# Forget-gate sums of a forgetting attention carried by the second score product, placed by DMA, in a hybrid decoder block

## The chip, the cores and the metric

One core of a Trainium2 chip runs the whole layer. The metric is the device time of one execution in microseconds; lower is better. The engines are TensorE (PE in the profile, PEld for its weight loads), VectorE (DVE), ScalarE (ACT), GpSimd (POOL) and SyncE (SP), which issues all DMAs. The PE clock granted over the profiled execution was 0.996 of full speed.

## The reference

A layer of width 1024 over 512 tokens: an RMS norm, one input projection, three mixers (a gated linear recurrence, a "native sparse" attention NSA, a forgetting attention FOX), an output projection and the residual. In all score products head_dim is 64 and queries and keys are RMS-normalised per head. What the change touches is the FOX score:

```python
log_f = jax.nn.log_sigmoid(f_logits.astype(jnp.float32) + f_b.astype(jnp.float32))
c = jnp.cumsum(log_f, axis=1).transpose(0, 2, 1)
...
s = (jnp.einsum('bqhd,bshd->bhqs', qb, k).astype(jnp.float32) * ATTN_SCALE
     + cb[..., None] - c[:, :, None, :])
p = safe_softmax(s, mask)
```

The term of the query's own position, cb, is the same for all keys of a row and falls out of the softmax; the kernel adds only the keys' term, minus c.

## The kernel before, in words

**Projections.** The input weights come in 39 chunks of 128 output channels (`CHUNKS`), the output weights in 12 more. SP loads each into a ring of three (`raw`, `load_w`, L435), ACT rounds it to float32r (`wh`, L552), DVE writes the remainder (`wl = raw - wh`, `split_low`, L922), both in rings of four slots, three chunks ahead of PE. PE computes each chunk as three products over eight k tiles (L1351, L1352, L1355; the token-major value chunks L1318 to L1320). The three chunks vn0 to vn2 are one projection, which waits for the low split of all three. The order of chunks is a list; FOX's queries (fq), keys (fk) and values (vf) and the gate chunks zn follow after the NSA attention, the chunks zf after the FOX attention.

**Head norms.** For a query or key chunk ACT squares, PE averages over heads, ACT seeds the root and DVE finishes it (`norm`, L941 to L943). Then ACT writes the high part (L626) and DVE the low part (`low_parts`, L952). A head has 64 channels, so one half of the 128 partitions is its own: the tile `q_fox` holds high queries in that half and low queries in the other. For keys both `kh_fox` and `kl_fox` are filled in the own half, and SP copies each into the other half by DMA (`stack`, L445). One product with `kh_fox` then gives (high + low query) times high key, one with `kl_fox` the same times low key.

**The forget gates.** ACT writes the log gates of 8 heads beside the table `head_sel`; `forget_gates` on DVE (L979 to L987, in chunk zn1) sums them along the tokens and splits the sum into three bf16 parts in `c_parts`, at partitions 0, 32 and 64. `head_sel` (built by `attention_tables`, L1205 to L1208) has ones in the three rows of a head, so a third product of `head_sel` and `c_parts` adds the sum of a head to all rows of its scores.

**The attentions.** The work is cut into units: one head, one query tile of 128, n = (t+1) x 128 keys. Eight units, two heads by four tiles in the order t = 1, 2, 0, 0, 3, 1, 2, 3, are a pair; the NSA attention has eight pairs, FOX four. Per unit PE computes the scores (FOX: L1482, L1483, L1484; NSA: L1483, L1484) into one of four banks (`S_RING`), DVE adds the mask and finds the maximum (L1143), ACT the exponential (L721), DVE the reciprocal of the sums, POOL scales (`scale_probs`, L529), PE transposes five units later (L1492), ACT or DVE copies that back, and PE multiplies with the values (L1511). Scores of unit u wait for the exponential of unit u - 4.

**The order on SP.** One loop over c issues the load of chunk c once the low split of chunk c - 3 is done, and after it the stacking of chunk c - 6; what stands behind a wait in this queue waits with it.

**DVE around chunks nq1 and nq2** (81 to 95 us). After the second compress (`compress(1)`, L1426, which signals `cmp_prod`) DVE finishes the norm of nq1, splits weights, writes low queries, and runs steps of the recurrence (L1006 to L1011), all elementwise operations of 128x512 or 64x512. POOL has no work there; its next is the first scale of the NSA attention.

## Time and profile before

| | |
|---|---|
| the runs shown | 429.39, 430.83 and 1045.02 us, median 430.83 |
| profiled execution | 429.14 us, of which span 427.4 us |
| PE, DVE, ACT, POOL busy | 97%, 67%, 61%, 16% of the span |
| NSA attention | 138.7 to 202.1 us |
| FOX projections and norms | 202 to 300.6 us |
| FOX attention | 300.6 to 334.2 us |
| last projections, output | 334.2 to 427.4 us |

The page of the profile gives busy shares and the chain of work that ended last; the timeline gives each instruction's start and time; the waits say who released an idle engine. Matmuls overlap in the records: the distance between two starts says more than their durations. A busy PE is therefore not PE at its peak.

### The profile page before, as it was taken

Reading aid. Unit: us, or ns where it says so; the run is one execution under the profiler, and the core shown is the slowest. Engines: PE = TensorE matmul, PEld = TensorE weight load, DVE = VectorE, ACT = ScalarE, POOL = GpSimd, SP = SyncE. Lnnn points to the kernel's source line nnn. Section 1 sums busy time; section 2 is a strip of 40 time slices with the busy share of each in tenths; the row PEclk is TensorE's granted clock in tenths of the full one; section 3 lists DMA queues with packets and bytes.
Section 4 is the critical chain, followed back from the end, with each engine's and each line's share of the span. In section 5 each row is a group of like instructions: output and inputs, shape, how many; then the busy total and the mean of one; then the engine's idle time right before and its main releaser. Section 6 shows DMA issues by size and latency. Waiting matters only on the chain.

```text
span 427.4 us, 6574 instructions
## 1 busy us (share of the span) xinstructions
PE 416.0 (97%) x2254; PEld 327.7 (77%) x2254; DVE 287.2 (67%) x616; ACT 258.8 (61%) x514; POOL 67.4 (16%) x125
## 2 busy tenths in 40 slices
PE   6999999999999899998999999999999999999996
PEld 4876788779888766665777987988776688888885
DVE  4667759988898876766268846799877389522205
ACT  5746996686565887885187778751877654311100
POOL 6000000000000656566000000000465200000000
PEclk9999999999999999999999999999999999999999
DMA  8912544421122000001112333641300115822005
GB/s 284 338 72 97 152 114 108 121 76 38 55 95 99 2 2 1 1 2 61 43 55 89 100 98 117 180 133 66 99 2 2 49 51 181 278 99 83 2 0 196
DMA packets 12385, 38.89 MB, mean 91 GB/s; under 512 B 1728, under 2 KB 1984, under 8 KB 12096
## 3 DMA queue, kind: packets, MB, share of 16 engines
q1 hardware_dynamic: 12352, 38.47, 28.0%
q8 instruction: 18, 0.29, 0.3%
q14 instruction: 15, 0.12, 0.1%
HBM read 32.17 MB, written 2.10 MB: 80 GB/s over the span
## 4 chain that ended last, share of the span: by engine, by line
PE 83%; DVE 9%; issue 2%; ACT 2%; POOL 2%; DMA 1%; SPq 0%; ACTq 0%; DVEq 0%
PE bank L1351 12%; PE bank L1355 12%; PE bank L1352 12%; PE bank L1511 6%; PE bank L1492 6%; PE bank L1599 5%; PE bank L1600 5%; PE bank L1601 5%; PE bank L1483 3%; PE bank L1484 3%; PE bank L1405 2%; PE bank L1318 2%; PE bank L1320 2%; PE bank L1319 2%; DMA raw<-in_w_in 1%
## 5 line engine op out<-in xcount | busy, mean ns | idle before, releaser
L1351 PE MATMUL bank<-xh,wh 128*128 128x512 f32 x248 | 103.0, 415 | 0.6 <-DVE wl L922 0.6
L1355 PE MATMUL bank<-xh,wl 128*128 128x512 f32 x248 | 96.9, 391 | 0.0
L1352 PE MATMUL bank<-xl,wh 128*128 128x512 f32 x248 | 96.8, 390 | 0.0
L922 DVE TENSOR_TENSOR wl<-raw,wh 128x1024 fp32r<-128x1024 f32 (+1 forms) x51 | 61.5, 1207 | 37.0 <-ACT wh L552 36.6
L552 ACT ACTIVATE wh<-raw 128x1024 fp32r<-128x1024 f32 (+1 forms) x51 | 52.6, 1037 | 29.3 <-PE bank L1601 28.4
L1351 PEld LDWEIGHTS bank<-xh,wh 128*128 128x128 f32 x248 | 46.6, 188 | 15.9 <-issue 6.3
L1143 DVE CUSTOM_DVE_ANT_0 bank<-bank,mask_row 128x256 f32<-128x256 f32 (+3 forms) x96 | 46.8, 500 | 14.8 <-PE bank L1484 14.1
L1352 PEld LDWEIGHTS bank<-xl,wh 128*128 128x128 f32 x248 | 46.6, 188 | 11.5 <-issue 2.6
L1355 PEld LDWEIGHTS bank<-xh,wl 128*128 128x128 f32 x248 | 46.5, 188 | 10.1
L529 POOL TENSOR_SCALAR probs<-probs,rcp,gates 128x384 f32<-128x384 f32 (+3 forms) x44 | 28.4, 655 | 138.5 <-DVE rcp L1167 138.5
L721 ACT ACTIVATE probs<-bank,negmax 128x256 f32<-128x256 f32 (+3 forms) x64 | 33.6, 529 | 6.4 <-DVE negmax L1143 6.1
L1600 PE MATMUL bank<-wl,yh 128*128 128x512 f32 x96 | 37.4, 389 | 0.0
L1599 PE MATMUL bank<-wh,yh 128*128 128x512 f32 x96 | 37.4, 389 | 0.0
L1601 PE MATMUL bank<-wh,yl 128*128 128x512 f32 x96 | 37.4, 389 | 0.0
L731 ACT ACTIVATE pT<-bank 128x384 f32<-128x384 f32 (+1 forms) x48 | 26.1, 545 | 14.9 <-PE bank L1492 14.4
L1492 PE MATMUL bank<-cst,probs 128*128 128x128 f32 x160 | 28.5, 277 | 2.1 <-POOL probs L529 1.1
L1318 PE MATMUL bank<-wh,xh 128*128 128x256 f32 (+1 forms) x96 | 29.1, 303 | 0.0
L1319 PE MATMUL bank<-wl,xh 128*128 128x256 f32 (+1 forms) x96 | 27.6, 287 | 0.0
L1320 PE MATMUL bank<-wh,xl 128*128 128x256 f32 (+1 forms) x96 | 27.5, 287 | 0.0
L1483 PE MATMUL bank<-kh_nsa,q_nsa 128*128 128x256 f32 (+3 forms) x64 | 25.0, 393 | 0.6 <-ACT probs L721 0.6
L1492 PEld LDWEIGHTS bank<-cst,probs 128*128 128x128 f32 x160 | 18.5, 140 | 7.2 <-POOL probs L529 3.9
L1601 PEld LDWEIGHTS bank<-wh,yl 128*128 128x128 f32 x96 | 18.0, 188 | 3.8
(233 smaller groups left out, 764.6 us busy)
## 6 DMA issues: line engine op xcount, KB each, us to landing
raw<-in_w_in SPq DMA_DIRECT2D x36, 512.0 KB, 3.4
raw<-in_w_out SPq DMA_DIRECT2D x12, 512.0 KB, 3.4
x_raw<-in_xT SPq DMA_DIRECT2D x4, 512.0 KB, 7.1
x_res<-in_x_tok SPq DMA_DIRECT2D x1, 2048.0 KB, 9.5
out_y<-y_out SPq DMA_DIRECT2D x8, 256.0 KB, 2.2
raw<-in_w_in SPq DMA_DIRECT2D x3, 384.0 KB, 3.2
cmp_w_sb<-in_cmp_w SPq DMA_DIRECT2D x1, 1024.0 KB, 7.2
kh_fox<-kh_fox SPq DMA_DIRECT2D x8, 128.0 KB, 2.3
```

What stands on the lines that cost most here:

```text
L552: act.activation(wh[:, c % HL, 0:width(c)], raw[:, c % RAW, 0:width(c)], ACT.Copy).then_inc(wh_ready, 1)
L922: dve.tensor_tensor(wl[:, c % HL, cols], raw[:, c % RAW, cols], wh[:, c % HL, cols].bitcast(F32), ALU.subtract).then_inc(wl_ready, 1)
L1143: dve.tensor_tensor_reduce(scores, scores, mask_row[:, SEQ - n:], scale=-1.0, scalar=3.0e38, op0=ALU.add, op1=ALU.min, accum_out=negmax[:, ...
L1318: pe.matmul(dst, xh[:, k, toks], hi[:, k], start=(k == 0), stop=False)
L1351: pe.matmul(dst, hi, xh[:, k, :], start=(k == 0), stop=False)
L1352: pe.matmul(dst, hi, xl[:, k, :], start=False, stop=False)
L1355: mm = pe.matmul(dst, lo, xh[:, k, :], start=False, stop=(k == KT - 1))
L1483: pe.matmul(dst[:, 0:n], q, kh[:, 0:n], start=(group == "nsa"), stop=False)
L1492: mm = pe.transpose(PT[u % PTB][:, cols], probs_of(u, j * P, (j + 1) * P), ident)
L1599: pe.matmul(dst, yh[:, e, toks], wh[:, c % HL, cols], start=(e == 0), stop=False)
L1600: pe.matmul(dst, yh[:, e, toks], wl[:, c % HL, cols], start=False, stop=False)
L1601: mm = pe.matmul(dst, yl[:, e, toks], wh[:, c % HL, cols], start=False, stop=(e == ET - 1))
```

## The change

The separate product of `head_sel` and `c_parts` in a FOX unit goes. The sums are now split into three float32r parts in `c_rows`. In the second product the moving tile `kl_fox` keeps low keys in the head's own half; its other half is zeros but for three rows, which hold the head's three sums. The stationary side is no longer `q_fox` but a second tile with the high query in its own half and, in the other, ones in those three rows and zeros elsewhere. So low query times low key is no longer computed.

The second query tile of heads 0 and 1 (and later 6 and 7) is the new `q_first`; heads 2 to 5 use slots 1 and 2 of the weight ring `wl`, which are free between chunks zn2 and zn3 and the chunks zf2 and zf3. POOL fills zeros and ones by copies of one column: eight fills of `kl_fox`, four of `q_first`, after `cmp_prod` reaches 2. SP copies the queries (`place_queries`) and the sums (`place_c`, eight DMAs of three rows, stepping 32 partitions in `c_rows`); low keys of FOX are no longer stacked. PE waits for `c_placed` in place of `c_ready` and for `q_placed` at each pair's first unit.

```diff
@@
 OUT_ORDER = (2, 1, 0, 3)
+Q_SLOT = {1: N_IN - 2, 2: N_IN - 1}
 STACK_LAG = 6
...
         ones = mask_row[:, SEQ - P:]
-        head_sel_f = sb("head_sel_f", [P, HEADS * P], BF16)
-        head_sel = head_sel_f[0:96, :].rearrange("p (h q) -> p h q", h=HEADS)
-        log_f = head_sel_f[96:96 + HEADS, :].bitcast(F32)
-        c_parts = sb("c_parts", [96, SEQ], BF16)
+        c_rows = sb("c_rows", [P, SEQ], F32R)
+        log_f = c_rows[96:96 + HEADS, :].bitcast(F32)
         rstd_bc = sb("rstd_bc", [P, SEQ])
...
                 kl_fox = sb("kl_fox", [P, HEADS, SEQ], F32R, m)
+                q_first = sb("q_first", [P, 2, SEQ], F32R, m)
             with ExitStack() as m:
...
-            return sum(0 if CHUNKS[x][0] in ("nq", "fq") else 4 for x in NORMED[:c])
+            return sum({"nq": 0, "fq": 0, "fk": 2}.get(CHUNKS[x][0], 4) for x in NORMED[:c])
...
             return slice(s * HD, (s + 1) * HD)
+        def const_rows(s):
+            return slice((1 - s) * HD, (1 - s) * HD + 3)
+        def query_and_ones(h):
+            if h // 2 in Q_SLOT:
+                return wl[:, Q_SLOT[h // 2] % HL, h % 2 * SEQ:(h % 2 + 1) * SEQ]
+            return q_first[:, h % 2, :]
...
             return q_fox[:, h, :], kh_fox[:, h, :], kl_fox[:, h, :]
+        def low_query(u):
+            group, h, _, _ = unit(u)
+            return query_and_ones(h) if group == "fox" else q_nsa[:, h, :]
...
                     own, other = half_of(s), half_of(1 - s)
-                    for plane in key_planes(c, s):
+                    planes = key_planes(c, s)
+                    for plane in planes[:1] if CHUNKS[c][0] == "fk" else planes:
                         sp.dma_start(plane[other, :].bitcast(F32), plane[own, :].bitcast(F32)).then_inc(stacked, 16)
+            def place_queries(i):
+                sp.wait_ge(h_ready, 2 * nth_normed(AT["fq", i]) + 2)
+                if i == 0:
+                    sp.wait_ge(cmp_prod, 2)
+                elif i in Q_SLOT:
+                    sp.wait_ge(fox_consts, HEADS + 4)
+                    sp.wait_ge(proj_done, proj_units(Q_SLOT[i] - HL + 1))
+                else:
+                    sp.wait_ge(s_ready, NSA_UNITS + PAIR_UNITS)
+                for s in range(2):
+                    own, other = half_of(s), half_of(1 - s)
+                    dst = query_and_ones(2 * i + s)
+                    sp.dma_start(dst[own, :].bitcast(F32), q_fox[own, 2 * i + s, :].bitcast(F32)).then_inc(q_placed[i], 16)
+                    if i in Q_SLOT:
+                        sp.dma_start(dst[other, :].bitcast(F32), q_first[other, s, :].bitcast(F32)).then_inc(q_placed[i], 16)
+            def place_c():
+                sp.wait_ge(c_ready, 1)
+                sp.wait_ge(fox_consts, HEADS)
+                for h in range(HEADS):
+                    sp.dma_start(kl_fox[const_rows(h % 2), h, :].bitcast(F32),
+                                 c_rows[h:h + 65:32, :].bitcast(F32)).then_inc(c_placed, 16)
...
             for c in range(4, N_STREAM + 6):
+                if c == N_IN - 1:
+                    place_c()
                 load_w(c)
+                if c == N_IN:
+                    for i in range(1, HEADS // 2):
+                        place_queries(i)
                 k = c - 5
...
                     stack(k)
+                if k == AT["fq", 0]:
+                    place_queries(0)
                 if c == N_IN + 4:
...
             pool.wait_ge(sel_set, NT + 1)
-            nc.gpsimd.memset(c_parts[:, :], 0.0)
             nc.gpsimd.memset(k_cmp[:, :, :], 0.0)
...
+            def fill(dst, rows, src):
+                return nc.gpsimd.tensor_copy(dst[rows, :], src[rows, 0:1].broadcast_to([rows.stop - rows.start, SEQ]))
+            def zeros_and_ones(h):
+                s = h % 2
+                fill(query_and_ones(h), half_of(1 - s), mask_row).then_inc(fox_consts, 1)
+                pool.wait_ge(fox_consts, HEADS + 2 * h + 1)
+                fill(query_and_ones(h), const_rows(s), one1).then_inc(fox_consts, 1)
+            pool.wait_ge(cmp_prod, 2)
+            for h in range(HEADS):
+                fill(kl_fox[:, h, :], half_of(1 - h % 2), mask_row).then_inc(fox_consts, 1)
+            zeros_and_ones(0)
+            zeros_and_ones(1)
             pool.wait_ge(gates_ready, 1)
...
                 one, b = std[96:96 + HEADS, :], work[0:HEADS, :]
-                mid = std[0:HEADS, :].bitcast(BF16)[:, 0:SEQ]
+                mid = std[0:HEADS, :].bitcast(F32R)
                 dve.wait_ge(normed, len(NORMED))
                 link(dve.tensor_tensor_scan(b, one, log_f, 0.0, ALU.mult, ALU.subtract))
-                dve.wait_ge(small_consts, 2)
-                link(dve.tensor_copy(c_parts[0:HEADS, :], b))
-                link(dve.tensor_tensor(b, b, c_parts[0:HEADS, :], ALU.subtract))
+                link(dve.tensor_copy(c_rows[0:HEADS, :], b))
+                link(dve.tensor_tensor(b, b, c_rows[0:HEADS, :].bitcast(F32), ALU.subtract))
                 link(dve.tensor_copy(mid, b))
-                link(dve.tensor_tensor(b, b, mid, ALU.subtract))
-                dve.tensor_copy(c_parts[32:32 + HEADS, :], mid)
-                dve.tensor_copy(c_parts[64:64 + HEADS, :], b).then_inc(c_ready, 1)
+                link(dve.tensor_tensor(b, b, mid.bitcast(F32), ALU.subtract))
+                dve.tensor_copy(c_rows[32:32 + HEADS, :], mid.bitcast(F32))
+                dve.tensor_copy(c_rows[64:64 + HEADS, :], b).then_inc(c_ready, 1)
...
-                sel = work[0:96, 0:HEADS]
-                link(dve.tensor_tensor(sel, cst[0:96, IDENT:IDENT + HEADS], cst[0:96, IDENT + 32:IDENT + 32 + HEADS],
-                                       ALU.add))
-                link(dve.tensor_tensor(sel, sel, cst[0:96, IDENT + 64:IDENT + 64 + HEADS], ALU.add))
-                dve.tensor_copy(head_sel[:, :, :],
-                                sel.unsqueeze(2).broadcast_to([96, HEADS, P])).then_inc(sel_ready, 1)
                 dve.tensor_copy(mask_row[:, SEQ - P:], cst[:, CAUSAL:CAUSAL + P])
...
                 dst, q = SCORE[u % S_RING], q[:, t * P:(t + 1) * P]
-                if group == "fox":
-                    pe.matmul(dst[:, 0:n], head_sel[:, h, :], c_parts[:, 0:n], start=True, stop=False)
-                pe.matmul(dst[:, 0:n], q, kh[:, 0:n], start=(group == "nsa"), stop=False)
-                pe.matmul(dst[:, 0:n], q, kl[:, 0:n], start=False, stop=True).then_inc(s_ready, 1)
+                if group == "fox" and u % PAIR_UNITS == 0:
+                    pe.wait_ge(q_placed[h // 2], 16 * (4 if h // 2 in Q_SLOT else 2))
+                pe.matmul(dst[:, 0:n], q, kh[:, 0:n], start=True, stop=False)
+                pe.matmul(dst[:, 0:n], low_query(u)[:, t * P:(t + 1) * P], kl[:, 0:n],
+                          start=False, stop=True).then_inc(s_ready, 1)
...
             pe.wait_ge(normed, len(NORMED))
-            pe.wait_ge(c_ready, 1)
+            pe.wait_ge(c_placed, 16 * HEADS)
+            pe.wait_ge(fox_consts, HEADS + 4)
             attention(NSA_UNITS, UNITS)
```

GpSimd behind the last of the small memsets, before:

```order
L509 MEMSET kv_pair 128x2x512
L513 COPY kv_pair<-chn 128x16 [waits chan_loaded,pe_placed]
L513 COPY kv_pair<-chn 128x16
L520 MEMSET u_pad 128x3 [waits x_sq_act,x_sq,xl_ready]
L520 MEMSET u_pad 128x3 x3
L529 TENSOR_SCALAR probs<-probs,rcp,gates 128x256 [waits rcp_ready,gates_ready]
```

and with the change, at the same place (`mask_row` is zero in its first column, `small` holds the one):

```order
L568 MEMSET u_pad 128x3 [waits x_sq_act,x_sq,xl_ready]
L568 MEMSET u_pad 128x3 x3
L583 CAST kl_fox<-mask_row 64x512 [waits cmp_prod]
L583 CAST kl_fox<-mask_row 64x512 x7
L583 CAST q_first<-mask_row 64x512
L583 CAST q_first<-small 3x512 [waits fox_consts]
L583 CAST q_first<-mask_row 64x512
L583 CAST q_first<-small 3x512 [waits fox_consts]
L577 TENSOR_SCALAR probs<-probs,rcp,gates 128x256 [waits rcp_ready,gates_ready]
```

Twelve casts now stand between the pads of the recurrence and the first scale; they wait only for the second compress.

SyncE from the stacking of the last key chunk to the loads behind the FOX attention, before:

```order
L445 DMA kh_fox<-kh_fox 64x512
L445 DMA kl_fox<-kl_fox 64x512
L435 DMA raw<-in_w_in 128x1024 [waits wl_ready] x4
L435 DMA raw<-in_w_out 128x1024 [waits wl_ready] x5
L479 DMA x_res<-in_x_tok 128x4096 [waits proj_done]
```

and with the change:

```order
L451 DMA raw<-in_w_in 128x1024 [waits wl_ready] x3
L486 DMA kl_fox<-c_rows 3x512 [waits fox_consts,c_ready]
L486 DMA kl_fox<-c_rows 3x512 x7
L451 DMA raw<-in_w_in 128x1024 [waits wl_ready]
L451 DMA raw<-in_w_out 128x1024 [waits wl_ready]
L477 DMA wl<-q_fox 64x512 [waits proj_done,fox_consts,h_ready]
L479 DMA wl<-q_first 64x512
L477 DMA wl<-q_fox 64x512
L479 DMA wl<-q_first 64x512
...
L477 DMA q_first<-q_fox 64x512 [waits s_ready,h_ready]
L477 DMA q_first<-q_fox 64x512
L451 DMA raw<-in_w_out 128x1024 [waits wl_ready] x4
```

The eight small copies stand ahead of the last load of input weights, the copies of queries behind the first load of output weights.

TensorE at the first two units of the FOX attention, before:

```order
L1482 MATMUL bank<-c_parts,head_sel_f 128x256 [waits c_ready,normed,p_ready,stacked,l_ready]
L1483 MATMUL bank<-kh_fox,q_fox 128x256
L1484 MATMUL bank<-kl_fox,q_fox 128x256
L1482 MATMUL bank<-c_parts,head_sel_f 128x384 [waits p_ready]
L1483 MATMUL bank<-kh_fox,q_fox 128x384
```

and with the change:

```order
L1411 MATMUL bank<-xh,wl 128x512
L1539 MATMUL bank<-kh_fox,q_fox 128x256 [waits fox_consts,c_placed,p_ready,normed,q_placed0,stacked,l_ready]
L1540 MATMUL bank<-kl_fox,q_first 128x256
L1539 MATMUL bank<-kh_fox,q_fox 128x384 [waits p_ready]
L1540 MATMUL bank<-kl_fox,q_first 128x384
```

A unit has two products instead of three, and the first one waits for the DMAs.

## Rows read from the trace of the kernel before

**Rows 1.** The page, part 4: the chain that ended last, shares by engine.

```profile
PE 83%; DVE 9%; issue 2%; ACT 2%; POOL 2%; DMA 1%; SPq 0%; ACTq 0%; DVEq 0%
```

**Rows 2.** Busy time by stretch: length, PE, PEld, DVE, ACT, POOL, clock, DMA.

```profile
45.00:90.00 45.00, 45.00 (x203) 35.76 (x196) 35.33 (x54) 35.93 (x57) 0.00 (x0) 1.00 0.44 120
...
317.90:326.50 8.60, 8.60 (x62) 6.30 (x61) 6.22 (x26) 6.36 (x21) 4.78 (x8) 1.00 0.00 0
```

**Rows 3.** The bias product by line: ns min/median/max, first and last start, forms.

```profile
L1482 PE MATMUL bank<-c_parts,head_sel_f x32: 222/305/389, 300.6 to 328.7; 96*128 96x256 bf16 x8, 96*128 96x384 bf16 x8, 96*128 96x128 bf16 x8, 96*128 96x512 bf16 x8
```

**Rows 4.** Chain in order of time: start, share, what; a product of 512 columns.

```profile
309.67 0.23 PE bank L1484
```

**Rows 5.** Timeline of PE: start us, us; first products of pairs, and two last ones.

```profile
143.61 0.36 PE L1483 MATMUL bank<-kh_nsa,q_nsa 128*128 128x256 f32 x1
...
151.17 0.39 PE L1483 MATMUL bank<-kh_nsa,q_nsa 128*128 128x256 f32 x1
...
157.12 0.48 PE L1483 MATMUL bank<-kh_nsa,q_nsa 128*128 128x512 f32 x1
...
158.88 0.39 PE L1483 MATMUL bank<-kh_nsa,q_nsa 128*128 128x256 f32 x1
...
300.66 0.36 PE L1483 MATMUL bank<-kh_fox,q_fox 128*128 128x256 f32 x1
...
305.98 0.36 PE L1483 MATMUL bank<-kh_fox,q_fox 128*128 128x256 f32 x1
...
313.53 0.37 PE L1483 MATMUL bank<-kh_fox,q_fox 128*128 128x256 f32 x1
...
322.10 0.37 PE L1483 MATMUL bank<-kh_fox,q_fox 128*128 128x256 f32 x1
...
328.77 0.58 PE L1483 MATMUL bank<-kh_fox,q_fox 128*128 128x512 f32 x1
```

**Rows 6.** Waits, 143.6 to 200 us: us in total, times, longest.

```profile
PEld bank L1483 <- ACT probs L721: 3.9, 8, 0.8
```

**Rows 7.** Timeline of DVE and POOL, 331 to 333 us; POOL's forms in 309.4 to 326.5.

```profile
331.31 0.69 DVE L1105 TENSOR_TENSOR qr<-qr,sq 128x512 f32<-128x512 f32 x1
331.49 1.04 POOL L529 TENSOR_SCALAR work<-work,rcp,small 128x384 f32<-128x384 f32 x1 [0.65 <-DVE rcp L1167]
332.03 1.03 DVE L1107 TENSOR_TENSOR o_nsa<-qr,o_nsa 128x512 f32<-128x512 f32 x1
...
L529 POOL TENSOR_SCALAR probs<-probs,rcp,small 128x384 f32<-128x384 f32 x4 | 2.6, 661 | 2.3 <-DVE rcp L1167 2.3
L529 POOL TENSOR_SCALAR probs<-probs,rcp,small 128x512 f32<-128x512 f32 x3 | 2.3, 767 | 0.7 <-DVE rcp L1167 0.7
```

**Rows 8.** Timeline: the last product of the compress, DVE behind it, the vn projection.

```profile
80.92 0.34 PE L1426 MATMUL bank<-kv_pair,cmp_w_sb 128*128 128x96 f32 x1
...
81.45 0.75 DVE L943 SCALAR_TENSOR_TENSOR qr<-qr,chn,std 128x512 f32<-128x512 f32 x1
...
85.97 1.22 DVE L1011 TENSOR_TENSOR_SCAN u_pad<-tau,ig 128x512 f32<-128x512 f32 x1
88.17 0.69 DVE L899 TENSOR_TENSOR qr<-bank,rstd_bc 128x512 f32<-128x512 f32 x1 [0.97 <-PE bank L1355]
...
93.65 0.96 DVE L922 TENSOR_TENSOR wl<-raw,wh 128x768 fp32r<-128x768 f32 x1
...
94.67 0.40 PE L1318 MATMUL bank<-wh,xh 128*128 128x288 f32 x1
```

**Rows 9.** Timeline of DVE: the end of the forget sums, the first FOX reduction.

```profile
295.38 0.42 DVE L987 CAST c_parts<-work 8x512 bf16<-8x512 f32 x1
...
301.43 0.42 DVE L1143 CUSTOM_DVE_ANT_0 bank<-bank,mask_row 128x256 f32<-128x256 f32 x1
```

**Rows 10.** SP's timeline at a stacking; DMA issues: KB each, us to landing.

```profile
249.03 0.60 SPq L445 DMA_DIRECT2D kh_fox<-kh_fox  x1
249.67 0.60 SPq L445 DMA_DIRECT2D kl_fox<-kl_fox  x1
...
kl_fox<-kl_fox SPq DMA_DIRECT2D x8, 128.0 KB, 2.3
```

More of the change, by code:

```diff
@@ L220, in program @@
         lam_act, csp_ready = sem("lam_act"), sem("csp_ready")
-        zl_sig, zl_done, sel_ready = sem("zl_sig"), sem("zl_done"), sem("sel_ready")
+        zl_sig, zl_done = sem("zl_sig"), sem("zl_done")
         ones_ready = sem("ones_ready")
@@ L232, in program @@
         sq_ready, norm_mean, norm_seed = sem("sq_ready"), sem("norm_mean"), sem("norm_seed")
+        c_placed, q_placed, fox_consts = sem("c_placed"), [sem(f"q_placed{i}") for i in range(HEADS // 2)], sem("fox_consts")
         normed, h_ready, l_ready, stacked = sem("normed"), sem("h_ready"), sem("l_ready"), sem("stacked")
@@ L676, in place_log @@
                 act.wait_ge(log_T, 1)
-                act.wait_ge(sel_ready, 1)
                 for t in range(NT):
```

## The prediction

> **What bounds the kernel now.** I read the page first: its chain of work that ended last lies to 83% on PE [rows 1], so a microsecond counts where PE waits or where PE's own work shrinks. Then the busy times by stretch. In a pair of the forgetting attention (317.9 to 326.5 us) PE is busy throughout while DVE, ACT and POOL are busy 6.2, 6.4 and 4.8 of 8.6 us; between 45 and 90 us PE is busy throughout and POOL does nothing [rows 2]. So the attention is near PE's limit, but three quarters of the way to ACT's, and every stall put into the projections before it is paid in full.
>
> **The attention: what goes.** Thirty-two bf16 matmuls, one ahead of each fox unit's two float32r products, are removed [rows 3]. They cover 8 x 20 x 128 / 2 = 10,240 columns (a pair's eight units have 20 blocks of 128, four pairs); a product of 512 columns holds the chain 0.23 us [rows 4], so PE's own saving is at most 20 x 0.23 = 4.6 us. The least is nothing. The kernel holds its own measurement of what is left: the NSA units do exactly what a fox unit will do (two products, same tiles, same transposes, values, reductions, exponentials). Starts of a pair's first product: NSA 143.61, 151.17, 158.88, so 7.56 and then 7.71; fox 300.66, 305.98, 313.53, 322.10, so 5.32, 7.55 and 8.57 [rows 5]. The first two fox stretches are filling, set by DVE, ACT and POOL, and already at NSA's pace: gain 0. The third gives 8.57 - 7.71 = 0.86. From the first to the last product of the last pair fox takes 328.77 - 322.10 = 6.67 and NSA 157.12 - 151.17 = 5.95: 0.72. Sum 1.6 us gained of the 4.6. What is late next is the ring of four score banks: in six NSA pairs PE's loads waited 3.9 us for the exponential that frees one [rows 6]. I take 1.6; ends 0 and 4.6.
>
> **The fills on POOL: the largest term.** Twelve casts of up to 64x512 are put on POOL behind cmp_prod, that is from about 81.3 us, when the second compress ends. POOL is idle there, so by itself this costs nothing; nor is any later POOL work late (the first scale waits until after 140 us). But the fills read and write SBUF while DVE runs through operations with two SBUF inputs. The trace shows what such pairs do to each other: at 331.31 DVE multiplies two SBUF tiles; POOL's 128x384 scale issued at 331.49 takes 1.04 us instead of 0.66, and the next DVE product, issued at 332.03, takes 1.03 instead of 0.69 [rows 7]. So each POOL read holds such a DVE operation by about 0.34 us for 384 elements, 0.34 x 512 / 384 = 0.45 for 512, and they alternate. POOL's fill should run between its 384 and 512 forms, 0.66 to 0.77 us [rows 7].
>
> Where it lands: from 81.45 to 87.19 us DVE runs seven such operations (L943, L922, L952 twice, L1009, L1010, L1011), then idles 0.97 us until PE has finished chunk nq2 [rows 8]. Seven fills delay it 7 x 0.45 = 3.2, of which the idle takes 0.97: 2.2 pass through. Of the five fills left, three find operations with one SBUF input (L899, L1023, L941, 1.7 us in all), two delay L942 and L943: 0.9. From 88.17 on DVE runs without a gap to the low split of chunk vn2 at 93.65, which ends at 94.61, and PE starts the vn projection, which needs it, at 94.67 [rows 8]: no slack at all. So 2.2 + 0.9 = 3.1, taken as 3.0, go straight into PE's chain; nothing behind it gives them back, since DVE and PE shift together. The ends: 0, if a cast that reads one column of a tile does not hold DVE; and if POOL's twelve go through in one row with DVE standing, the whole time of 12 x about 0.6 = 7.2, less 0.97, is 6.3 us.
>
> The Trainium skill (SBUF — State Buffer, section "Who interferes with whom") says the pair of ports that both engines share is an exclusive lock, taken for the whole instruction, when DVE has two SBUF inputs and GpSimd reads SBUF. The trace agrees that one blocks the other, but not on the length: 0.34 us of an operation of 0.66. With whole instructions the nine delays would be about 0.66 each, 5.9 less 0.97, so 5 us in place of 3.0. The same section says a GpSimd instruction that only writes does not contend; the memset of c_parts that goes is of that kind and is worth nothing here.
>
> **The sums' way to PE.** Before, DVE wrote c_parts in place at 295.38 + 0.42 = 295.80 [rows 9], and PE's first fox unit came at 300.66 [rows 5]. Now the last sum is about 0.13 later (a float32 copy in place of a bf16 one of 0.28), then SP issues eight DMAs of 3 x 512, and PE waits for all eight. SP's copies within SBUF start 0.64 us apart and land 2.3 us after issue [rows 10]. No row shows one of three partitions. If it costs as much, the eighth issues at 295.95 + 7 x 0.64 = 300.4 and lands at 302.7: PE stands 2.1 us. Since DVE's first reduction starts only at 301.43 [rows 9], some 0.4 after its scores, the attention itself slips 1.7. If issues take half and landing 2.0, the eighth lands at 300.2 and it is 0. I take 1.3, nearer the row; ends 0 and 2.1.
>
> Behind place_c in SP's queue stand the loads of chunk 38 and of the first w_out chunk. They leave 1 to 3 us later, but are not read before the next split after the attention, some 30 us on: free. Behind them stand the four copies for heads 2 and 3, with one megabyte of loads ahead of them in the same queues. Issued from about 302.3 in steps of 0.64, the last leaves at 304.2 and lands at 306.5; the second pair, at 305.98 before, is now due near 307. Close, so I charge 0.3 us (ends 0 and 1). Heads 4 and 5 are due 7 us later, heads 6 and 7 sixteen: free. place_queries(0) waits for the high parts of fq0, which ACT writes before DVE's low split that the next load needs anyway: free. The next weight load, of w_out 1, waits for a split after the attention: SP's new wait for the first pair's scores costs it nothing. Eight stacking copies of the low keys go; PE did not wait for them: nothing. On DVE the three operations that built head_sel, near 47 us, go, 1 us at most under a PE that is busy throughout there [rows 2]: nothing.
>
> **Sum.** +3.0 (fills) + 1.3 (sums) + 0.3 (queries) - 1.6 (matmuls) = +3.0 us. The profiled execution took 429.14 us (427.4 of span and 1.7 around it), so it would be 432.1. Two of the three runs shown took 429.39 and 430.83, the third, 1045.02, stands alone; their middle is 430.1, 0.7 below the median, and 430.1 + 3.0 gives 433.1. I say 433.0.
>
> **Rivals.** (A) Not slower: the fills cost nothing. The place is DVE at 81.3 to 88.2 us; the mechanism is that POOL's casts from a single broadcast column read little, or that POOL always yields, so that DVE is held less than the 0.97 us of idle ahead of 88.17. From that point on the term is 0 and the sum is 0.0: 430.1, and if the placement is cheap too, 428.5. For it: no row shows a cast with such a source, and a delay of under 0.14 per fill would do. Against it: [rows 7]. (B) POOL wins the port each time, since its next fill is queued when DVE's operation asks; the term is 6.3 instead of 3.0: 436.4. For it: eight fills have no wait among them. Against: in [rows 7] the two take turns. The skill's rule on whole instructions leads to about the same place, 435.1. (C) The attention is PE-bound and gives the whole 4.6: 430.1 again, by another way. Against it: ACT needs 6.4 of the 7.4 us that would be left per pair and NSA pairs stall on it [rows 2, 6]. (D) The placements are late by more than their rows say (eight small copies and four queries behind a megabyte of loads), 3 us more: 436.1. For it: each has one semaphore and PE waits for the last. Against: copies of 128 KB land in 2.3 us.
>
> **How the numbers follow.** Forecast 0.40, A 0.25, B 0.18, C 0.07, D 0.10. The forecast's own range is 431.5 to 434.5. A and C reach down to 428.5 and 430, B and D up to 436.4, both together to 439.5. From 429.0 to 437.0 leaves out the lower tail of A and the sum of B and D, under 0.2. Two per cent, about what a measurement of this kernel can tell from no change, is 8.6 us: slower by more needs B and D together (439.5), 0.06; faster by more would need 422, beyond the 4.6 us that are there, 0.02; within it 0.92.
>
> **What would show it.** Right: POOL fills at 81 to 90 us with DVE operations of two SBUF inputs at 1.1 instead of 0.69 us beside them; DVE's idle of 0.97 gone; PE standing some 3 us in all before 98 us, and the vn projection starting near 97.7 instead of 94.67. Attention: PE idle 1 to 2 us before the first fox unit with c_placed as releaser; fox pairs 7.7 apart in the third stretch. Wrong: vn starting at 94.7 (A), fox pairs at 7.3 (C), DVE operations of several us beside the fills (B), or PE waiting for a DMA at the start of the second pair by more than a microsecond (D).

## The result, and the profile after

| | before | after |
|---|---|---|
| median of 6 runs each, us | 430.36 | 433.05 |
| lowest to highest of the six, us | 429.39 to 1045.02 | 432.35 to 433.65 |
| profiled execution: time, span, us | 429.14, 427.4 | 433.3, 431.5 |
| granted clock, mean over the profiled span | 0.996 | 0.984 |

The ratio after to before is 1.0073, with the 95% interval 1.0055 to 1.0092: about 3 us slower (the interval is 2.4 to 4.0 us), within the 2% called no change. The run of 1045.02 us stands alone and has no known cause; without it the median before is 430.29, and the medians are 2.8 us apart. The forecast was 433.0. The total came out, and none of its four terms did: the fills were put too high, the sums, the queries and the gain too low. First the chain of the page, which stays on PE [rows 1], with 4% of issue where 2% stood:

```profile
PE 82%; DVE 8%; issue 4%; ACT 2%; POOL 2%; DMA 1%; POOLq 0%; SPq 0%; ACTq 0%; DVEq 0%
```

The main reading is PE's timeline (start in us, length, line, operation, in brackets the idle time before it and its releaser):

```profile
94.60 0.28 PE L1607 MATMUL bank<-cst,v_cmp 64*32 64x64 f32 x2
96.64 0.40 PE L1374 MATMUL bank<-wh,xh 128*128 128x288 f32 x1 [1.75 <-DVE wl L985]
...
141.46 0.36 PE L1539 MATMUL bank<-kh_nsa,q_nsa 128*128 128x256 f32 x1
...
303.14 0.39 PE L1411 MATMUL bank<-xh,wl 128*128 128x512 f32 x1
305.83 0.55 PE L1539 MATMUL bank<-kh_fox,q_fox 128*128 128x256 f32 x1 [2.30 <-issue]
...
312.52 0.35 PE L1539 MATMUL bank<-kh_fox,q_fox 128*128 128x256 f32 x1
...
319.27 0.39 PE L1539 MATMUL bank<-kh_fox,q_fox 128*128 128x256 f32 x1
...
326.98 0.39 PE L1539 MATMUL bank<-kh_fox,q_fox 128*128 128x256 f32 x1
...
332.92 0.48 PE L1539 MATMUL bank<-kh_fox,q_fox 128*128 128x512 f32 x1
```

Set beside [rows 5, 8] it gives the whole account. The vn projection starts at 96.64 instead of 94.67, +1.97. The first fox product comes at 305.83 instead of 300.66, +5.17. The stretches between pairs are 6.69, 6.75 and 7.71 instead of 5.32, 7.55 and 8.57, and the last pair takes 5.94 instead of 6.67. That is +5.17 +1.37 -0.80 -0.86 -0.73 = +4.15, and the span grew by 4.1. The two profiled executions, 429.14 and 433.3 us, lie further apart than the ratio says, so these terms add up to more than its 3.1 us. And 0.2 us of the 4.15 were there before the first fill: DVE starts L1006 at 81.64, and the same operation started at 81.45 before [rows 8].

The first product of the NSA attention, at 141.46 above, stood here before:

```profile
138.71 0.36 PE L1483 MATMUL bank<-kh_nsa,q_nsa 128*128 128x256 f32 x1
```

So NSA starts 2.75 us late.

Both new stalls stand there: 1.75 us ahead of vn, released by DVE's low split, and 2.30 us ahead of the first fox unit. The second has the releaser "issue", that is, nothing the profile knows of. The wait that the change puts there is c_placed, whose DMAs have no landing in the trace; that it is this wait was tested below. DVE beside the fills, the same view:

```profile
81.64 1.03 DVE L1006 SCALAR_TENSOR_TENSOR qr<-qr,chn,std 128x512 f32<-128x512 f32 x1
82.60 1.36 DVE L985 TENSOR_TENSOR wl<-raw,wh 128x768 fp32r<-128x768 f32 x1
83.99 2.00 DVE L1015 TENSOR_TENSOR q_nsa<-qr,q_nsa 64x512 fp32r<-64x512 f32 x2
86.02 0.99 DVE L1071 SCALAR_TENSOR_TENSOR tau<-tau,xc 128x512 f32<-128x512 f32 x1
87.05 0.98 DVE L1072 SCALAR_TENSOR_TENSOR ig<-ig,xc 128x512 f32<-128x512 f32 x1
88.06 1.52 DVE L1073 TENSOR_TENSOR_SCAN u_pad<-tau,ig 128x512 f32<-128x512 f32 x1
89.50 0.66 DVE L962 TENSOR_TENSOR qr<-bank,rstd_bc 128x512 f32<-128x512 f32 x1
...
298.27 0.42 DVE L1049 CAST c_rows<-work 8x512 fp32r<-8x512 f32 x1
```

and POOL in the same stretch:

```profile
81.52 8.47 POOL L583 CAST kl_fox<-mask_row 64x512 fp32r<-64x512 f32 x8 [64.37 <-PE bank L1482]
90.05 0.62 POOL L583 CAST q_first<-mask_row 64x512 fp32r<-64x512 f32 x1
...
91.40 0.95 POOL L583 CAST q_first<-mask_row 64x512 fp32r<-64x512 f32 x1
```

Each engine holds the other and they take turns. A fill of 0.62 us alone takes 0.95 beside such an operation, and the first eight took 0.61 to 1.42 each, 8.47 us with the steps between them. L1006 takes 1.03 at 81.64 where it took 0.75 [rows 8], and the scan 1.52 where it took 1.22: 0.3 us each. The idle of 0.97 us ahead of the next L962 [rows 8] is gone.

The granted clock, after, by stretch (length, then busy us of PE, PEld, DVE, ACT, POOL, then clock, DMA share, GB/s):

```profile
98.00:100.00 2.00, 2.00 (x10) 2.00 (x9) 1.93 (x4) 0.63 (x1) 0.00 (x0) 0.50 0.58 227
...
306.00:312.00 6.00, 5.93 (x21) 5.01 (x22) 4.04 (x18) 3.76 (x14) 2.44 (x5) 0.50 1.04 296
```

Behind each of the two stalls PE ran for a while at the lower of its two levels, 1.2 GHz: some 3.4 us behind the first, some 6.8 us behind the second. SP's timeline after the forget sums:

```profile
298.72 5.64 SPq L486 DMA_DIRECT2D kl_fox<-c_rows  x8
304.40 0.42 SPq L451 DMA_DIRECT2D raw<-in_w_in  x1
304.87 0.42 SPq L451 DMA_DIRECT2D raw<-in_w_out  x1
305.41 0.52 SPq L477 DMA_DIRECT2D wl<-q_fox  x1
305.97 0.59 SPq L479 DMA_DIRECT2D wl<-q_first  x1
...
307.25 0.60 SPq L479 DMA_DIRECT2D wl<-q_first  x1
```

The last sum ends at 298.69, eight placements take 5.64 us to issue, 0.71 apart, the last at about 303.7, and PE starts 2.1 us after it. Copies for heads 2 and 3 leave between 305.41 and 307.85, behind two loads of 512 KB. From issue to landing (DMA issues from 297 to 320 us; KB each, median us) they take twice what a stacking copy took [rows 10]:

```profile
wl<-q_first SPq DMA_DIRECT2D x4, 128.0 KB, 4.7
```

### The profile page after: what moved, and what is told of

Its sections match the earlier page's. It is cut to its first block, busy times and chain, and to the rows that moved or that the text cites. A ratio compares the mean times of both kernels' runs of the same rounds, so it can differ in the third digit from the quotient of the medians.

```text
span 431.5 us, 6537 instructions
## 1 busy us (share of the span) xinstructions
PE 416.4 (96%) x2222; PEld 327.5 (76%) x2222; DVE 288.5 (67%) x613; ACT 259.1 (60%) x514; POOL 78.5 (18%) x136
## 4 chain that ended last, share of the span: by engine, by line
PE 82%; DVE 8%; issue 4%; ACT 2%; POOL 2%; DMA 1%; POOLq 0%; SPq 0%; ACTq 0%; DVEq 0%
PE bank L1407 12%; PE bank L1411 11%; PE bank L1408 11%; PE bank L1568 6%; PE bank L1549 6%; PE bank L1659 5%; PE bank L1657 5%; PE bank L1658 5%; PE bank L1539 3%; PE bank L1374 3%; PE bank L1376 3%; PE bank L1375 3%; PE bank L1540 3%; PE bank L1461 2%; DMA raw<-in_w_in 1%
## 5 line engine op out<-in xcount | busy, mean ns | idle before, releaser
L577 POOL TENSOR_SCALAR work<-work,rcp,small 128x256 f32<-128x256 f32 (+3 forms) x6 | 4.0, 675 | 108.3 <-DVE rcp L1229 108.3
```

## The experiments

Runs of the first four experiments were made on one chip, the next four on a second, the last two on a third. Each ratio is to the kernel before on its own chip.

**e1: the bias product alone taken out of the kernel before.** The forget term is left out of the scores.

```
-                if group == "fox":
-                    pe.matmul(dst[:, 0:n], head_sel[:, h, :], c_parts[:, 0:n], start=True, stop=False)
-                pe.matmul(dst[:, 0:n], q, kh[:, 0:n], start=(group == "nsa"), stop=False)
+                pe.matmul(dst[:, 0:n], q, kh[:, 0:n], start=True, stop=False)
```

> The kernel before, only the product of head_sel and c_parts left out of every FOX unit, so the forget term is missing from the scores; nothing is placed or filled. It isolates the term I put at 1.6 us. The theory that the ring of score banks and ACT bound what is left expects 427.9 to 428.8 us against about 430.4 of before, fox pairs 7.7 us apart in the third stretch. The rival, attention bound by PE, expects 4.6 us less, 425.8, and pairs 7.4 apart.

Measured 427.14 against 429.53 us, ratio 0.9949 [0.9931, 0.9967], so 2.2 to 2.4 us by times. Its PE timeline:

```profile
300.62 0.28 PE L1481 MATMUL bank<-kh_fox,q_fox 128*128 128x256 f32 x1
...
305.57 0.36 PE L1481 MATMUL bank<-kh_fox,q_fox 128*128 128x256 f32 x1
...
312.62 0.38 PE L1481 MATMUL bank<-kh_fox,q_fox 128*128 128x256 f32 x1
...
320.32 0.39 PE L1481 MATMUL bank<-kh_fox,q_fox 128*128 128x256 f32 x1
...
326.27 0.48 PE L1481 MATMUL bank<-kh_fox,q_fox 128*128 128x512 f32 x1
```

4.95, 7.05, 7.70, and 5.95 for the last pair. The last two are what NSA foretold (7.71 and 5.95). The first two, which the prediction held to be set by the other engines, gave 0.37 and 0.50. Together 2.5 us, not the 4.6 that PE's own saving could at most have been.

The change also gives the second product another stationary tile. That costs nothing that shows: the changed kernel has 7.71 and 5.94 where e1, which kept `q_fox` in both products, has 7.70 and 5.95.

**e2: the fills alone, put into the kernel before.** It has q_first, twelve casts and the wait of the fk stacking for them, and no other part of the change. Its last four casts all fill 64 rows; in the change two of them fill three rows.

```
             pool.wait_ge(cmp_prod, 2)
+            for h in range(HEADS):
+                fill(kl_fox[:, h, :], half_of(1 - h % 2), mask_row).then_inc(fox_consts, 1)
+            for n in range(4):
+                fill(q_first[:, n // 2, :], half_of(n % 2), mask_row).then_inc(fox_consts, 1)
...
```

> The kernel before plus twelve casts of 64x512 on POOL behind the second compress, eight into the halves of kl_fox that the stacking later overwrites and four into a tile that nobody reads. It isolates the fills. The port theory expects DVE operations with two SBUF inputs 0.3 to 0.45 us longer beside them, the vn projection about 2 us late and, since PE then runs 3.4 us at half clock as it does in the changed kernel, 2.5 to 3 us in all: 433. The rival that the fills are harmless and vn is late through something else in the change expects 430.4 and vn at 94.7 us.

431.85 against 429.53, ratio 1.0050 [1.0032, 1.0067]: +2.2 us. In its profile vn starts at 96.64 as in the changed kernel; the clock falls behind the stall there too (0.50 from 98 to 101 us), and the first FOX unit is 2.7 us late in this one execution. Of the 2.5 to 3 us that were expected 2.2 came.

**e3: the placements on two queues.** Changed kernel, heads 4 to 7 issued by ACT.

```
-                for h in range(HEADS):
+                for h in range(HEADS // 2):
...
+                if c == FIRST_Z + 2:
+                    act.wait_ge(c_ready, 1)
+                    for h in range(HEADS // 2, HEADS):
+                        act.dma_start(kl_fox[const_rows(h % 2), h, :].bitcast(F32),
+                                      c_rows[h:h + 65:32, :].bitcast(F32)).then_inc(c_placed, 16)
```

> The changed kernel with the eight small copies of sums issued half from SP and half from ScalarE, whose queue is idle there. My theory is that PE's 2.3 us wait before the first fox unit is the issue time of eight DMAs at 0.64 each: with four per queue the last leaves near 300.7 and lands before 303.4, the wait is gone and so is the half clock of 6.8 us after it: 429.5 to 430.5 us against 433.05 of the changed kernel. The rival, that the landing of such a three-row copy is slow by itself or that both queues share one issuer, expects at most 1 us less and a wait of over 1 us still there.

432.56 against 429.53, ratio 1.0070 [1.0052, 1.0087], no better than the change. SP's and ACT's timelines:

```profile
298.32 2.90 SPq L486 DMA_DIRECT2D kl_fox<-c_rows  x4
301.27 0.42 SPq L451 DMA_DIRECT2D raw<-in_w_in  x1
```

```profile
298.33 3.75 ACTq L913 DMA_DIRECT2D kl_fox<-c_rows  x4
```

SP was done in half the time, but PE still stood 2.07 us, so the expectation of 429.5 to 430.5 us failed. Side by side the issues took 0.72 and 0.94 us each, and the load of 512 KB left at 301.27, at about the time of ACT's last copy. By an estimate that copy left near 301.1 (298.33 + 3 x 0.94), and PE went on at 305.21, 4.1 us after it; in the changed kernel PE went on 2.1 us after the last copy. So the stall is not issue time alone. That the load delays those copies is the likely reason; it is not shown, since no trace has their landing. The queries of the second pair left some 2 us earlier than in the changed kernel, and the second pair started 5.7 us after the first instead of 6.7.

**e4: the fills as memsets.** Changed kernel, write only.

```
-                return nc.gpsimd.tensor_copy(dst[rows, :], src[rows, 0:1].broadcast_to([rows.stop - rows.start, SEQ]))
+                return nc.gpsimd.memset(dst[rows, :].bitcast(F32), value)
```

> The changed kernel with the twelve fills as memsets, which write SBUF and read nothing, instead of casts of one column. If the shared thing is what both engines read through, DVE's operations beside them take 0.69 us again, the vn projection starts near 94.8 us at full clock, and the time is 2.3 to 2.8 us below the changed kernel: 430.4. If any POOL access of SBUF holds DVE, or the delay has another cause, vn is as late as before (96.6) and the time stays at 433.

431.10 against 429.53, ratio 1.0035 [1.0021, 1.0049], half the loss of the changed kernel: 1.6 us less by the ratios, where 2.3 to 2.8 had been expected. DVE beside the memsets (which run from 82.55 to 89.40, this execution being 1.2 us late from its first 15 us on):

```profile
84.33 1.39 DVE L1015 TENSOR_TENSOR q_nsa<-qr,q_nsa 64x512 fp32r<-64x512 f32 x2
85.75 0.69 DVE L1071 SCALAR_TENSOR_TENSOR tau<-tau,xc 128x512 f32<-128x512 f32 x1
...
89.39 0.69 DVE L962 TENSOR_TENSOR qr<-bank,rstd_bc 128x512 f32<-128x512 f32 x1 [0.97 <-PE bank L1411]
```

Every operation has its old length, the idle 0.97 is back, and PE does not stand at vn, which starts at 95.89, late by those 1.2 us and nothing more. What cost time was that the casts read SBUF, not that POOL was busy.

**e5: PE kept busy until the placements land.** Eleven products into a bank that nothing reads yet, ahead of the wait for c_placed.

```
+            pe.wait_ge(log_placed, NT)
+            for i in range(11):
+                pe.matmul(PT[0][:, :], wh[:, (FOX_END - 1) % HL, 0:P], xh[:, 0, :], start=True, stop=True)
             pe.wait_ge(c_placed, 16 * HEADS)
```

> The changed kernel with eleven idle products of 512 columns in TensorE's queue ahead of its wait for the sums, into a bank that nobody needs there; they fill the 2.3 us in which it stood. The first fox unit comes no earlier. The theory that the idle stretch costs twice, once as a wait and once by the 3.4 or 6.8 us at half clock behind it, expects full clock from the first fox unit on, the second pair 5 us after the first instead of 6.7, and 1.0 to 1.7 us less than the changed kernel. The rival, that the slow first pair is the wait for the copied queries of heads 2 and 3, expects the second pair no sooner and the time unchanged.

434.28 against 429.69, ratio 1.0097 [1.0076, 1.0119]. The clock stayed at 1.00 from 303 to 315 us, and the pairs came no earlier:

```profile
303.06 2.66 PE L1635 MATMUL bank<-xh,wh 128*128 128x512 f32 x11
...
312.72 0.36 PE L1539 MATMUL bank<-kh_fox,q_fox 128*128 128x256 f32 x1 [2.34 <-DMA wl<-q_first]
```

So full clock gained nothing in the first pair: what the half clock had filled became an open wait for the queries of the second pair. Two profiles of the changed kernel agree that those queries set its start. The last of their copies is issued at 307.25 in the one and at 306.55 in the other (e8 below), and the second pair starts 5.27 us after it in both, though the low clock lasted twice as long in the first. The time was not unchanged, as the rival had it: it is 1.5 us above that of e8 on the same chip. In the profile the query copies take 5.4 us to land instead of 4.7; why the kernel is slower stays open.

**e6 and e7: placements and queries in the order of use.** Each pair gets its own semaphore; SP issues the sums of pairs 0 and 1, the queries of pair 1, the sums of pairs 2 and 3, then the loads. e7 is that on the changed kernel, e6 has the memsets of e4 besides.

```
-                    place_c()
+                    place_c((0, 1))
+                    place_queries(1)
+                    place_c((2, 3))
...
+                    pe.wait_ge(c_placed[h // 2], 32)
```

> The changed kernel with three edits: fills as memsets; the sums of each pair of heads on a semaphore of their own, awaited at that pair; and in SyncE's queue the sums of heads 0 to 3 first, then the queries of heads 2 and 3, then the other sums, all before the loads. If fills, sums and queries are the whole loss, it comes to the kernel before without the bias product: no stall at vn, none at the first fox unit, pairs as there, 2.0 to 2.6 us faster than the kernel before (about 427.3 against 429.5). If the second pair still waits for its queries, 1 to 1.5 us of that is missing.

> The same order of placements and split semaphores, but with the casts of the changed kernel. Against the one with memsets it should show the fills alone once more: vn near 96.6 us and 2.0 to 2.8 us more, so about the time of the kernel before. If the effects overlap (PE's delay at vn giving SyncE and DVE time that helps later), the difference is under 1.5.

e6: 427.42 against 429.69, ratio 0.9950 [0.9929, 0.9970]. e7: 429.90, ratio 0.9999 [0.9983, 1.0015]. They differ only in the fills: 2.5 us by the medians, 2.1 by the ratios, as in e2. The new order takes the other 2.9 us (3.2 by the ratios) off the changed kernel (e8 below, 432.75). In e7's profile vn starts at 97.78 and not near 96.6, but 1.15 us of that were there before the first fill. In e6's profile the third pair, whose queries still stood behind the loads, now waited:

```profile
314.83 0.36 PE L1542 MATMUL bank<-kh_fox,q_fox 128*128 128x256 f32 x1 [1.51 <-DMA wl<-q_first]
```

**e8: the changed kernel again**, on the chip of e5 to e7, without an edit.

> The changed kernel itself, to have it beside the others on the same chip: 0.6 to 0.9% above the kernel before, a stall of about 2 us at vn and another before the first fox unit, both in every profile if they belong to the mechanism and not to one execution.

432.75 against 429.69, ratio 1.0074 [1.0051, 1.0098]. This execution kept its clock at 1.00 behind the stall at vn (96.69, NSA from 140.74), and the low clock in the attention lasted half as long. Its FOX starts:

```profile
305.11 0.36 PE L1539 MATMUL bank<-kh_fox,q_fox 128*128 128x256 f32 x1 [2.30 <-issue]
...
311.82 0.36 PE L1539 MATMUL bank<-kh_fox,q_fox 128*128 128x256 f32 x1 [0.83 <-DMA wl<-q_first]
```

The first pair again takes 6.7 us, now partly as an open wait for the queries.

**e9: also the queries of pair 2 ahead of the loads**, on e6, with only the sums of pair 0 ahead of the first queries; and **e10: the queries of pairs 1 and 2 ahead of the loads in the changed kernel**, the eight placements as they were. The edit of e10:

```
                     place_c()
+                    place_queries(1)
+                    place_queries(2)
                 load_w(c)
```

> The reordered kernel with memsets, now with the queries of heads 4 and 5 also ahead of both weight loads (order: sums of pair 0, queries 1, sums 1, queries 2, sums 2 and 3, loads, queries 3). In its predecessor the third pair stood 1.5 us until a copy into wl had landed. If that is a copy waiting behind a megabyte of loads, the third pair now starts 7.0 to 7.2 us after the second instead of 8.6, and the time is 1.2 to 1.6 us below 427.4 for a before of 429.7: ratio 0.991. If copies within SBUF are slow when many are in flight, whatever loads there are, the wait stays and the ratio is 0.995 again.

> The changed kernel with one edit: the queries of pairs 1 and 2 are placed right behind the sums, ahead of the two loads. The first fox unit is as late as before (2.3 us wait). If the second pair was late because its copies land behind the loads, it now starts 5 to 5.7 us after the first instead of 6.7, and 1.0 to 1.7 us are gained: ratio 1.004 against 1.007. If the half clock sets the second pair's start, it stays at 6.7 and the ratio at 1.007.

e9: 426.93 against 429.11, ratio 0.9953 [0.9936, 0.9970]. No wait for a DMA is left in the attention, and its pairs come as in e1, which had no sums and no queries to place at all:

```profile
300.86 0.28 PE L1543 MATMUL bank<-kh_fox,q_fox 128*128 128x256 f32 x1
...
305.80 0.36 PE L1543 MATMUL bank<-kh_fox,q_fox 128*128 128x256 f32 x1
```

By times it is not better than e6, and the ratio of 0.991 that was expected did not come: the profiled execution of e6 took 1.5 us more than e6's median, so the wait in it is not shown for the other runs. e10: 431.87 against 429.11, ratio 1.0064 [1.0042, 1.0086]. Its second pair starts 5.67 us after the first instead of 6.7, its query copies land in 2.3 us instead of 4.7, and PE still stands 2.30 us before the first. Against e8 the median is 0.9 us lower on another chip, whose kernel before was 0.6 lower; the intervals overlap widely, so the time alone decides nothing here. Of the 5.67 us some 0.7 are still more than e1's 4.95, though the last query copy of the pair was issued at 307.08 and these copies land in 2.3 us, well ahead of the pair at 312.28. There the clock was 0.50 from 309 to 312 us. So where no DMA is awaited, the half clock seems to cost about that much; it is one profile.

e6 and e9 are faster than the kernel before by some 0.5%; their intervals leave out 1, and both lie within the 2% called no change.

## Why the prediction was right in sum and wrong in its terms

| term, us | predicted | profile after | by experiments |
|---|---|---|---|
| fills | +3.0 | +2.0 at vn, +2.75 at NSA | +2.2 (e2), +2.1 to 2.5 (e7 less e6), +1.6 (change less e4) |
| sums' way to PE | +1.3 | +2.42 | sums and queries together +2.9 to 3.2 (e8 less e7) |
| queries | +0.3 | +1.44 | |
| matmuls removed | -1.6 | -2.46 | -2.2 to -2.4 (e1) |
| sum | +3.0 | +4.15 | time +3.1 [2.4, 4.0] |

The profile's 2.42 for the sums is 5.17 less the 2.75 by which NSA was late; its 1.44 for the queries is the second pair's 6.69 less e1's 4.95, less the 0.3 that the next stretch (6.75 against 7.05) gives back. The matmuls' 2.46 is what e1's profile gained. The last column of fills compares e4 with the change by their ratios.

**Fills.** The mechanism was right and the size not. The step that failed is "0.34 x 512 / 384 = 0.45": the hold did not grow with the columns of the fill. It is 0.3 us an operation, as in [rows 7] (0.4 at the two 128x768 splits). The fill took 0.62 us alone, not the 0.66 to 0.77 that was expected, so it is about as long as the 384-column scale of [rows 7], and whether a longer instruction would hold longer is not shown. Seven operations beside the eight first fills (the pair of L1015 counted twice) were held 0.28 + 0.41 + 0.61 + 0.30 + 0.29 + 0.30 = 2.2 us, less the idle of 0.97, and two more 0.6: 1.85, where 3.0 was said. Rival A is out, since the idle was used up, and so is B, since the two engines took turns in the changed kernel. By the Trainium skill (SBUF — State Buffer, section "SBUF: two separate sides") the lock holds for the whole instruction. One after the other, a DVE operation of 0.69 us and a fill of 0.62 would take 1.31 us; the operations at 86.02, 87.05 and 88.06 start 1.03 and 1.01 us apart. So the recorded lengths overlap by 0.3 us, and on these the trace disagrees; whether a part of each recorded length lies outside the lock, no run shows. The Trainium skill also says on that page (section "Who interferes with whom") that a GpSimd instruction that only writes does not contend. There e4 agrees: 0.69 us beside memsets.

What brought the term back up is a cost that the prediction did not have. Behind the stall at vn the clock fell to 0.50 from about 97.4 to 100.8, and NSA starts 2.75 late instead of 2.0. It does not come in each execution. Of the seven profiles with this stall, three have the low clock behind it (the changed kernel, e2, e5) and need 44.8 us from vn to the first NSA product; the four others (e3, e7, e8, e10) need 44.0 to 44.1, as the kernel before does (94.67 to 138.71). So where it comes it costs 0.75 us. The stall before the first FOX unit was followed by 3.4 us at low clock in four profiles (e3, e4, e8, e10) and by 6.8 in the changed kernel's, and in the profiles without that stall there is none.

The mean clocks of the other runs do not tell where a low stretch was. By an estimate 3.4 us at half clock take 3.4 x 0.5 / 430 = 0.004 off the mean. Each profile, that of the kernel before too, has one such stretch in its first 15 us; those of e4, e7 and e10 have two there, and are 1.0 to 1.5 us later than the changed kernel's at the first fill. Of 53 runs of the kernel before beside the experiments, 42 have a mean clock of 0.994 or more (median span 427.4 us) and 11 have 0.991 or 0.992 (428.7). Of the 12 runs of the changed kernel none is in the first class; seven have 0.991 or 0.992 (median 430.6) and five 0.988 or less (431.8). That it always loses at least one stretch more fits the stall before the first FOX unit. How much of the 3.1 us the clock makes is not separated, and why some executions fall at vn and others don't stays open.

**Sums.** The mechanism was right and the size too small: 1.3 was taken between 0 and 2.1, and 2.4 came. The step that failed is the middle value, the hope that three partitions issue or land faster than 128 KB. They cost 0.71 us each, 6 KB for a little more than the price of 128, and PE went on 7.1 us after the last sum, where the end of "if it costs as much" has 6.75. The 0.4 us that were taken off because DVE's first reduction starts late did not appear: PE stood 2.30 and the attention slipped 2.4. That the delay is this placement is shown by e6, e7 and e9, where PE waits for two of the eight at first and its stall is gone. In e3 a second queue, with a load between, did not help.

**Queries.** The step "the last leaves at 304.2 and lands at 306.5", with its charge of 0.3, failed, and mainly in the landing. Counted from the last sum, which itself came 2.75 us later through the fills, the last copy left after 8.6 us where 8.25 was said, but landed in 4.7 us, not 2.3, behind one megabyte of loads (DMA share 1.04 between 306 and 312). Rival D's mechanism was thus real: the sums and queries cost 3.9 us in the profile (2.9 to 3.2 by times) where 1.6 was said, short of the 4.6 that D asked. That PE "waits for a DMA at the start of the second pair" was named as its sign; the profile after hid it behind the low clock, and e5 (2.34 us) and e8 (0.83 us) brought it out. e10 shows the price of the loads: with the queries ahead of them their copies land in 2.3 us and the pair takes 5.7.

**Matmuls.** Right in the third stretch (7.71 as said) and in the last pair (0.73 against 0.72). The step that failed is "the first two fox stretches are filling, set by DVE, ACT and POOL ... gain 0", inferred from likeness to NSA's 7.56. e1 gave 0.37 and 0.50. The same trace had the answer for the first stretch: NSA's own first pair runs from 138.71 to 143.61, 4.90 us, and 5.32 less 4.90 is 0.42. The prediction compared fox's first stretches with NSA's second and third. Nor do the busy times say that the other engines set those stretches: in the kernel before PE was busy 5.47 of the 6 us from 300 to 306, DVE 4.56, ACT 4.63 and POOL 2.20. Rival C's 4.6 is out.

So fills were 0.5 to 1.4 us too dear by times, and the gain 0.6 to 0.8 too small; sums and queries were 1.3 to 2.3 too cheap. These cancelled, and that the total came out at 433.0 was luck. What had the best grounds beforehand was what came from the same work elsewhere in the same trace, NSA's pace.

## What to carry to other kernels

What removing PE work pays can be read from another stage of the same kernel that already runs without it, if like is set beside like: first pair beside first pair. Count DMAs, not bytes, when small rows are placed just before they are needed; issue them in the order of use, with a semaphore for each consumer, and ahead of loads that nobody awaits yet. Take the landing time from copies that stand behind the same loads, not from copies that stand alone. A constant fill on POOL belongs in a write-only instruction, or away from DVE operations with two SBUF inputs.

## What the runs showed of the hardware that was not expected

- A copy of 3 rows of 2 KB within SBUF took SP 0.71 us to issue, one of 128 KB 0.60; with ACT's queue issuing too, 0.72 and 0.94 each.
- Two instructions on SBUF, both reading it (DVE 0.69 us, POOL 0.62), held each other by about 0.3 us each, with a fill of 512 columns as with a scale of 384 of nearly the same length, and a memset not at all.
- A stall of 1.7 us at vn was followed by 3.4 us at half clock in three of seven profiles; one of 2.1 to 2.3 us before the first FOX unit by 3.4 or 6.8 us in all five. At vn the low clock cost 0.75 us each time. In the first FOX pair e5's profile gained nothing from full clock, since a DMA was awaited next.
- Copies of 128 KB within SBUF landed in 2.3 us, and in 4.7 behind two loads of 512 KB.
- A wait that ends late can be invisible: "issue" stood for c_placed, and PE at half clock for the queries.
